# Six gather buffers and twelve weight slots in the place of eight and eight

## What is computed

```python
def _peer(x, w_q, sub_keys, u, v):
    q = (xt @ w_q).reshape(T, PEER_HEADS, 2, PEER_HALF)
    s = jnp.einsum('thpe,pne->thpn', q, sub_keys)
    top_s, top_i = lax.top_k(s, PEER_TOPK)
    cand = top_s[:, :, 0, :, None] + top_s[:, :, 1, None, :]
    best_s, best_j = lax.top_k(cand, PEER_TOPK)
    ...
    expert = idx_a * PEER_N_KEYS + idx_b
    gate = jax.nn.softmax(best_s, axis=-1)
    h = jnp.einsum('td,thkd->thk', xb, u[eb])
    a = jax.nn.gelu(h) * gb
    return jnp.einsum('thk,thkd->td', a, v[eb])
```

## Time and profile before

| | us |
|---|---|
| median of 3 runs | 2339.59 (2339.57 to 2340.19) |
| the profiled execution | 2333.25 |
| its span, first to last instruction | 2331.5 |
| PE busy | 2054.6 (88%) |
| DVE busy | 1327.9 (57%) |
| ACT, POOL busy | 808.7, 572.0 |
| granted TensorE clock | 0.954 |
| share of 16 DMA engines: gathers, weights | 56.8%, 21.1% |
| moved | 721.81 MB, mean 310 GB/s |

### The profile page before, as it was taken

How to read it: one execution, slowest core, us unless ns; L and a number is a source line. 1 busy time by engine, 2 the same in 40 slices (tenths; PEclk the granted TensorE clock), 3 DMA queues, 4 the chain that set the end, 5 groups by cost and what they waited for, 6 DMA issues and landing times.

```text
span 2331.5 us, 24718 instructions
## 1 busy us (share of the span) xinstructions
PE 2054.6 (88%) x7828; PEld 1250.4 (54%) x7828; DVE 1327.9 (57%) x2941; ACT 808.7 (35%) x2272; POOL 572.0 (25%) x530
## 2 busy tenths in 40 slices
PE   7999998999999759988789989887999988787776
PEld 6888865888565446633335654443666455332222
DVE  2613443899322346888873355589446558954444
ACT  1414331444321223333342363333336323433332
POOL 0000000000000023444443224333323434344332
PEclk9989968999999879998989999999999999899999
DMA  7532203455443259999999999999999999999997
GB/s 269 185 115 80 78 13 117 163 189 188 130 155 133 95 200 419 419 416 411 411 417 418 417 420 419 419 418 378 409 417 419 418 418 419 383 422 422 421 422 319
DMA packets 123943, 721.81 MB, mean 310 GB/s; under 512 B 13744, under 2 KB 13872, under 8 KB 58160
## 3 DMA queue, kind: packets, MB, share of 16 engines
q0 software_dynamic: 75584, 545.09, 56.8%
q1 hardware_dynamic: 47952, 174.19, 21.1%
q10 hardware_dynamic: 288, 1.05, 0.1%
HBM read 719.23 MB, written 1.05 MB: 309 GB/s over the span
## 4 chain that ended last, share of the span: by engine, by line
PE 29%; DMA 26%; DVE 11%; issue 4%; ACT 3%; POOL 2%; POOLq 0%; DVEq 0%; ACTq 0%; PEldq 0%
DMA arena<-peer_uv,arena 26%; PE bank L752 15%; PE bank L1082 13%; DVE arena L1775 4%; POOL arena L1626 2%; ACT arena L1529 1%; DVE arena L1756 1%; DVE arena L1754 1%; DVE arena L1757 1%; DVE arena L1722 0%; DVE arena L1714 0%; DVE arena L1716 0%; DVE x_tok L1693 0%; DVE x_tok L1695 0%; ACT arena L1522 0%
## 5 line engine op out<-in xcount | busy, mean ns | idle before, releaser
L1082 PE MATMUL bank<-arena 128*128 128x512 f32 x2048 | 991.3, 621 | 212.3 <-ACT arena L1529 211.6
L1775 DVE SCALAR_TENSOR_TENSOR arena<-arena,x_tok 128x1024 f32<-128x1024 f32 x512 | 619.4, 1224 | 529.8 <-DMA arena<-peer_uv,arena 527.1
L1626 POOL DMA_INDIRECT arena<-peer_uv,arena x512 | 555.5, 1085 | 937.2 <-PE bank L1082 829.1
L1082 PEld LDWEIGHTS bank<-arena 128*128 128x128 f32 x2048 | 374.7, 195 | 721.3 <-ACT arena L1529 383.9
L752 PE MATMUL bank<-xT,weight_ring 128*128 128x128 f32 (+2 forms) x2544 | 436.0, 328 | 5.5 <-DVE xT L1650 4.0
L752 PEld LDWEIGHTS bank<-xT,weight_ring 128*128 128x128 f32 (+1 forms) x2544 | 389.6, 191 | 84.8 <-issue 40.9
L1522 ACT ACTIVATE arena<-arena 128x1 f32<-128x1 f32 x512 | 103.3, 202 | 905.4 <-DVE arena L1775 904.4
L1516 ACT ACTIVATE arena<-const_tile,arena 128x128 f32<-128x128 f32 x512 | 198.0, 387 | 6.1 <-DVE arena L1767 6.1
L1529 ACT ACTIVATE arena<-arena 128x128 f32<-128x128 f32 x512 | 197.8, 386 | 0.6
L752 PE MATMUL bank<-arena 128*128 128x128 f32 (+10 forms) x888 | 164.9, 340 | 9.9 <-DVE arena L2138 4.9
L1264 ACT ACTIVATE arena<-bank 128x512 f32<-128x512 f32 (+6 forms) x164 | 78.6, 492 | 259.8 <-PE bank L752 259.8
(11 more groups left out here) (203 smaller groups left out, 1326.1 us busy)
## 6 DMA issues: line engine op xcount, KB each, us to landing
weight_ring<-weights SPq DMA_DIRECT2D x328, 512.0 KB, 4.4
arena<-peer_uv,arena POOLq DMA_INDIRECT x512, 14.9
row_ring<-rows_in POOLq DMA_DIRECT2D x10, 512.0 KB, 5.1
const_tile<-consts POOLq DMA_DIRECT2D x1, 1849.0 KB, 8.0
x_tok<-x_in SPq DMA_DIRECT2D x2, 512.0 KB, 4.8
memT<-memT_in POOLq DMA_DIRECT2D x1, 1024.0 KB, 11.2
row_ring<-rows_in ACTq DMA_DIRECT2D x2, 512.0 KB, 13.1
x_out<-x_tok SPq DMA_DIRECT2D x2, 512.0 KB, 5.7
```

The lines of the kernel that those rows point to most:

```text
L1082: ins = pe.matmul(b[:, :], diag[n % DIAGS], gbuf[n % GBUF][:, 1, h * 512:(h + 1) * 512], start=n % P == 0, stop=n % P == P - 1)
L1626: pool.indirect_dma_start(gbuf[n % GBUF].rearrange("p a d -> p (a d)"), None, peer_uv, bass.IndirectOffsetOnAxis(ap=expert[t][:, s:s + 1]. ...
L1775: dve.scalar_tensor_tensor(u, u, 1.0, x[:, t, :], ALU.mult, ALU.mult, accum_out=hdot[:, s:s + 1])\
```

## The change

`RING` goes from 8 to 12 and `GBUF` from 8 to 6. A gather buffer is 2048 columns and a ring slot 1024, so two buffers make four slots, and `ARENA` shrinks by 4096 columns. Since `lo` moves down by 4096, four tiles (`dqT`, `gate_diag`, `dkT` and their neighbours) that stood behind the other areas move into the room between `lo` + 7040 and `stat`; `diag` stays behind it.

```diff
-RING = 8
+RING = 12
...
-GBUF = 8
+GBUF = 6
...
-ARENA = 28752
+ARENA = 24656
...
-        assert lo + 7040 <= small + 1102
-        dqT = area(24016, 18, P)
-        diag = [area(26320 + 128 * b, P) for b in range(DIAGS)]
-        gate_diag = [area(26320 + 128 * DIAGS + 128 * b, P) for b in range(2)]
-        dkT = area(26576 + 128 * DIAGS, DSLOTS, S)
-        assert 26576 + 128 * DIAGS + 1536 == ARENA
+        assert lo + 11136 <= small + 1102
+        dqT = area(lo + 7040, 18, P)
+        diag = [area(24016 + 128 * b, P) for b in range(DIAGS)]
+        gate_diag = [area(lo + 10880 + 128 * b, P) for b in range(2)]
+        dkT = area(lo + 9344, DSLOTS, S)
+        assert 24016 + 128 * DIAGS == ARENA
```

## The result

The changed kernel takes 2383.77 us (median of 4 runs, 2375.61 to 2402.48), the kernel before in the same measurement 2339.88 us: 1.0199 times the time before, interval 1.0154 to 1.0245. The ratios on record are taken from the runs in the chip's faster state, the medians from all runs, so a ratio can lie beside the quotient of two medians (1.0188 here). By the medians the change is 43.9 us slower, 29 us above the forecast and outside its range. Its profiled execution took 2385.83 us, with a span of 2384.0 us against 2331.5.

What follows compares the result with a forecast made beforehand. PE and its chains bound the kernel before 848.5 us, gather bytes at some 419 GB/s plus idle DMA time after it. -9 + 0 + 10.5 + 0.5 + 10 + 3 = +15 us gave 2354.6 us, range 2335 to 2374.

Steps and rivals of the forecast that it cites:

- part 3: Second stretch, two gather buffers fewer: a loss from late consumers, in terms of +10.5, +0.5, +10 and +3 us.
- the reserve: Gather queue, last pass: time in flight beyond a gather's need, 9.2 us with eight buffers and 4.3 with six.
- rival D: Gather queue: starving costs more than the queue's arithmetic; all upper ends, +48 us, 2388, halfway 2371; chance 0.15.
- 3a: DVE routing parts come late and empty the gather queue: +10.5 us in pass 0, +0.5 in passes 1 and 2.
- 3b: Boundaries of passes 1|2 and 2|3: the queue is empty 5 us sooner at each, +10 us, ends +5 and +12.
- 3c: First 150 us after the first gather: DMA lacks at most the two gathers once, +3 us, ends 0 and +5.
- Part 1: Weight loads after the first gather: 123 instead of 131, 10.0 us of DMA; -9 us, ends -10 and -5.
- Part 2: Before the first gather at 848.5 us: a deeper weight ring saves nothing, 0 us, ends -1 and +2.
- The need of a gather: Gather queue: one gather needs 5.7 us, read from the first one, which had nothing ahead of it.
- 3a, parts of pass 0: After slot 42 of pass 0: 15 routing parts on DVE at 0.7 us each, +10.5 us, ends 0 and 30.
- 3a, parts of passes 1 and 2: Passes 1 and 2: reserve of 7.7 us exceeds any routing part; +0.5 us for all 24, ends 0 and 10.
- The named signs: Trace signs of being right: 324 loads, last pass about 10 us in flight, 1000 to 1190 about 390 GB/s, pass 0 +13 us.

Runs made afterwards that it cites:

- r6_g9: Nine gather buffers and a ring of six, against the kernel before with eight and eight: median 2331.65 us, ratio 0.9958.
- second profile: The changed kernel run and profiled once more, nothing altered: 2385.88 us in one run, second stretch 1533.4 us against 1531.1.
- fewheads_g6: Query blocks of heads 2 to 7 cut to two of eight matmuls, against six buffers with ring 8: idle DMA before slot 48 16.3 to 9.3 us.

## Why the prediction was wrong, point by point

**Sign and mechanism were right.** The loss is the gather queue running dry behind late consumers, in the second stretch, against which stand the 10 us of eight loads' bytes. What failed is the size of the terms of part 3: +15 became +48.2 us in the profile, beside +4.5 before the first gather. The step that failed is the reserve: the prediction gave a gather 5.7 us and so a late consumer 4.3 us of room, where the runs show 7.7 and 2.3, and it counted lateness in the first 150 us once. It is rival D by its number (all upper ends, +48, 2388), and by half of its reason: the last sixteenth of a gather among others does land 2 us late, but the last pass, where that would show first, kept its 421 GB/s. That the total met D's sum is luck, since its terms are others (3a +18.8 and +15.0 for 30 and 10, 3b +6.0 for 12, 3c +10.3 for 5, and 8.1 that it left out).

**Part 1, -9: right by count, uncertain by what it brought.** 8 loads fewer after the first gather, 10.0 us of bytes; measured by itself, with eight buffers, 1.03 us a load. With six buffers less may have come through where the loads are missing. Slots 320 to 384 take 189.4 and 189.7 us with a ring of twelve (10.4 and 10.3 idle) and 198.5, 193.3 and 194.4 us with six buffers and a ring of 8 (7.4, 4.1 and 4.5 idle). So the missing loads shorten this stretch by 4 to 9 us, and 3 to 6 us of the idle time in it are theirs: the bytes were gone, and the engines behind the queue did not come sooner. This is the prediction's "DVE would be just full" with its end of -5.

**Part 2, 0: right.** Nothing of the first stretch hangs on the ring; r6_g9, with a ring of six, has no loss either.

**The need of a gather, 5.7 us: wrong, and with it the reserve that 3a rests on.** It was read from the one gather with nothing beside it. The prediction then called 9.2 and 4.3 us the reserve; with 7.7 they are 7.3 and 2.3. A warning was in the earlier trace rows: 11.3 us from issue to landing in 1000 to 1190 us, less two cadences, is 6.1, already below 7.7.

**3a, parts of pass 0, +10.5: 18.8.** Two slips in one term. The prediction worked out a reserve of 0.4 for just this stretch and then held the parts against the last pass's 4.3. And it let PE work off waiting slots at 1.98 us, though the row of 1078.82 above (2.91 us, clock 0.50) was there to be read in the trace of the kernel before. Of its 15 parts 13 stand in this stretch: 1.45 us each, inside the range 0 to 30 for the term, near its middle.

**3a, parts of passes 1 and 2, +0.5: 15.0 (10.9 in the second profile).** The upper end was 10; some 3 to 6 us of the 15.0 belong to part 1, as said. The prediction had two reserves for the same stretch and took the larger: 5.1 from the median of 16.9 us, and 7.7 from a round of 6 x 3.05. Parts of 5 and 6 us fit into 7.7 and not into 5.1. And the median was from the whole of pass 1, which mixes its unhurried half (20.4 before 1480) with the routing itself: there it is 15.1 and 15.0. Issues of the kernel before by window, 1230:1480, 1490:1590 and 1890:1985 us:

```profile
arena<-peer_uv,arena POOLq DMA_INDIRECT x78, 20.4
```
```profile
arena<-peer_uv,arena POOLq DMA_INDIRECT x33, 15.1
```
```profile
arena<-peer_uv,arena POOLq DMA_INDIRECT x32, 15.0
```

Less two cadences of 3.0 that is 9.0, and above the measured need of 7.7 only 1.3 us are left for parts of 5 and 6 us. That this is what these stretches lose is worked out and not shown: no run left out their parts.

**3b, boundaries, +10: 6.0.** The queue was empty there with eight; two gathers fewer empty it sooner, but by 3 us a boundary, not by 5.

**3c, first 150 us, +3 (at most 5): 10.3, 13.3 in the second profile.** "At most the two gathers once" was false. The queue empties in two places of this stretch at least, by 3.2 and 4.4 us; `fewheads_g6` shows PE's blocks to be behind the first and some half of the whole.

**Left out, 0: 8.1.** 128 to 192, 272 to 320 and the last stretch, 2.4 to 2.9 us each. No run looks into them.

**The named signs.** 324 loads and 10 us from issue to dot in the last pass came true, so did the 421 GB/s there. 1000 to 1200 us came to 382 GB/s for "about 390", but pass 0 got 27.6 us longer (from first gather to slot 128) and not 13. "Passes 1 and 2 unchanged but for the boundaries" was false, and so was the first gather at 848.5.

**Open** is why the last part of a gather among others lands 2 us later than a lone gather's. At 420 GB/s its own bytes are 2.5 us, so it isn't plain sharing with one neighbour. Of the 8 KB packets the slowest in a hundred took 0.32 us in the last pass of both kernels, 0.47 before and 0.89 after the change in slots 48 to 128, and 1.13 with four buffers in the last pass: packets are longest where the queue runs dry. Which of the two brings about the other no run here shows.

## What to carry to other kernels

Cutting the depth of a queue is free until the reserve is gone, and then each step costs more than the last (11, 53, 100, 217 us here). So take the reserve stretch by stretch as the buffer's round less the need of a transfer among others (found in a run with too few buffers, not at the first lone transfer), and hold against it the longest block on each in-order engine, with PE's restart at a lower clock added. A price "once" for a late consumer has to be multiplied by how often one comes. Where two readings give two reserves for one stretch, as 5.1 and 7.7 did here, find out why before taking one.

## What was not expected of the hardware

**The first stretch varies by more than what was to be measured.** The first gather stands at 828.5 to 865.2 us in profiles of kernels whose first stretch is the same work, and the runs of the kernel before lie between 2313.38 and 2351.78 us (median 2338.58, 29 runs). The granted clock of TensorE does it. At 300 to 350 us, the kernel with nine buffers and the kernel before:

```profile
300.00:350.00 50.00, 45.31 (x244) 31.29 (x245) 30.71 (x74) 17.42 (x58) 4.35 (x1) 0.97 0.07 22
```
```profile
300.00:350.00 50.00, 46.74 (x167) 34.38 (x168) 23.70 (x58) 14.77 (x51) 4.25 (x1) 0.55 0.00 0
```

PE is about full in both; at 0.55, just above the lower of its two levels (1.2 of 2.4 GHz), it gets through 167 matmuls in the place of 244. Up to 305 us both kernels keep step within 0.1 us, and in both PE then starts after 3.23 us without work. The clock falls to half in both; in one it is back after 3.4 us, in the other after 51.2 us in which PE is busy throughout. At the first gather they are 20.0 us apart (828.5 and 848.5). No gather has run by then, so the change isn't in it. An effect in the second stretch is therefore read from first gather to end; medians of runs carry this spread with them, and a single run of the kernel before can lie 25 us beside its median.

**PE's short idle times are paid twice.** Where it had 4.3 us without work its granted clock was at half for 6.8 us, in both kernels: from 0.9 us after its restart at 1078.82 in the kernel before, and from 1.4 us ahead of its restart at 1048.09 in the changed one. A part of DVE that comes late is lengthened by it.
